# The last weight pair moves ahead of the overflow steps in a two-layer-trunk inference kernel

## Chip, core and metric

The kernel runs on one core of one Trainium2 chip. The metric is the device time in microseconds (us) of one execution; the time given for a kernel is the median of several runs. A profile is one more execution, in which the hardware records when each engine ran which instruction.

## What is computed

One inference step over 544 tokens (512 prompt tokens and 32 sample tokens, width 1024): a mixer sublayer (projections, chunk-wise spatial gating, a causal convolution with an RG-LRU scan, a sigmoid merge and an output projection), then a hierarchical mixture of experts, then a last RMS norm. The change concerns the experts:

```python
def hier_moe(x, w_rg, b_rg, w_re, b_re, w_gate, w_up, w_down):
    ...
    pg_top, g_idx = lax.top_k(pg, 1)          # one of 4 groups
    e_in = ...                                # logits of the 8 experts of that group
    pe_top, e_idx = lax.top_k(pe, TOP_K_INNER)   # 2 experts
    w = pg_top * pe_top / jnp.sum(pe_top, axis=-1, keepdims=True)
    ...
    h = jax.nn.silu(jnp.einsum('td,edf->tef', xf, w_gate)) * jnp.einsum('td,edf->tef', xf, w_up)
    h = h * gates.astype(h.dtype)[..., None]
    y = jnp.einsum('tef,efd->td', h, w_down)
```

There are 32 experts of width 256, and each token uses two of them: 1088 token places in all. The weights are float32, 3.1 MB for each expert.

## The kernel before

**Stages.** The first 375 us or so are the mixer; its weights are streamed in units and split into a high and a low part. Then the router works out on DVE (lines 1021 to 1136) which expert takes which token, and the rest of the kernel runs the experts.

**The steps of the expert stage.** Experts are run in pairs, 16 pairs (`PAIRS`) for 32 experts. A step takes a column of 128 token places: 64 (`CAP`) for the even expert, 64 for the odd one. On TensorE the two halves run side by side on 64 columns of the array each. Where an expert has more than 64 tokens, the rest goes into an extra step, in which one expert alone runs, in the first 64 places (`halves` is `(0,)`). `nx` is the number of extra steps; the router writes it and the experts concerned to `nxi`, and every engine loads it into a register once `extra_ready` is up. The column (number of the step) that a token goes to is worked out in the router: `epr` is the pair's, `xcnt[:, 2, :]` the first extra column of an expert. The extra steps stand before the last pair: columns 0 to 14 are pairs 0 to 14, columns 15 to 14 + `nx` the extras, and column 15 + `nx` is pair 15. Hence two DVE instructions (lines 1088 and 1090) add `nx` to the column of pair 15.

**One step** (`pair`, line 1437). TensorE waits for the transposed token rows `xgT` and the gate/up weights and multiplies (line 1445; 8 blocks of 128 in the contraction, the first four need part 0 of the weights, the last four part 1). With `next_rows` it then transposes the gathered rows `xg` of the next step (`transposes`, line 1429), which DVE copies to `xgT` (line 1143). Meanwhile ACT has worked out silu (line 748) and DVE the product `hm` (line 1148); TensorE transposes `hm` (line 1456), ACT copies `hT`, and TensorE multiplies with the down weights, part 2 (line 1466). ACT copies the sum to `yo` (line 753), and GpSimd scatters it by row to `ytok` in DRAM (line 553), after it has gathered the rows of the step after next (line 543). `yo` and `xg` are single buffers. Each float32 matmul of the program stands as two MATMULs in the trace.

**Weights.** There are three slots (`wslot[q]`), each of two halves (s = 0, 1), each half in three parts of 1 MB. The SP queue issues all weight transfers in the order of its program; before each part it waits until the step that uses that part of the slot is through with it: part 0 for `gu_half`, part 1 for `gu_mm`, part 2 for `pair_mm`. `refill(q, count, number)` brings two experts, `further` one. Pairs 0 to 14 use slots 0, 1, 2 in turn, the extras use half 0 of slot 0, and pair 15 slot 1. So the nine last transfers, with `nx` = 1, are: three for the extra (after pair 12 has freed slot 0), six for pair 15 (after pair 13 has freed slot 1).

**The end.** When the last scatter has landed (`yo_free`), SP loads all of `ytok` back in tiles, DVE adds them with the gates (line 1173), and the final norm and stores follow.

Of the kernel before, what the change touches and what calls it, by code (L numbers as in the profile page):

```python
# [22 lines left out]
P = 128  # L23
# [11 lines left out]
NE = NG * EG  # L35
# [4 lines left out]
PAIRS = NE // 2  # L40
# [19 lines left out]
ALU = mybir.AluOpType  # L60
# [37 lines left out]
def build(nc, x, wmix, wgate, chan, wst, bs, rows, wr, br, wmoe, y, vp, vs, st):  # L98
# [3 lines left out]
    def at(name, offset, shape, dt=F32):  # L102
# [7 lines left out]
    wslot = [[at(f"wslot{q}{s}", (first + s * 24) * K, [P, EW]) for s in range(2)]  # L110
             for q, first in enumerate((0, 97, 48))]
# [108 lines left out]
    T2 = 2 * TILES  # L220
# [4 lines left out]
    xcnt = small("xcnt", [P, 3, NE])  # L225
# [8 lines left out]
    with ExitStack() as ctx:  # L234
# [10 lines left out]
        part_in = [[[sem(f"part{n}_in{q}{s}") for s in range(2)] for q in range(3)] for n in range(3)]  # L245
# [117 lines left out]
        def _(sp_):  # L363
            e = sp_
# [68 lines left out]
            def refill(q, count, number):  # L433

                for part, used in enumerate((gu_half, gu_mm, pair_mm)):
                    lo, hi = PARTS[part]
                    e.wait_ge(used, count)
                    e.sem_inc(held, 1)
                    for s in range(2):
                        e.dma_start(wslot[q][s][:, lo:hi], wmoe[bass.ds(number + s, 1), :, lo:hi].rearrange(  # L440
                            "a p c -> (a p) c")).then_inc(part_in[part][q][s], 16)

            with e.Fori(0, 4) as i:
                for q in range(3):
                    refill(q, i * 3 + (q + 1), i * 6 + (6 + 2 * q))

            e.wait_ge(extra_ready, 1)
            nx = e.value_load(nxi[0:1, 0:1], min_val=0, max_val=EXTRA)

            def further(count, m):  # L450
                ex = e.value_load(nxi[0:1, bass.ds(m + 1, 1)], min_val=0, max_val=NE - 1)
                for part, used in enumerate((gu_half, gu_mm, pair_mm)):
                    lo, hi = PARTS[part]
                    e.wait_ge(used, count)
                    e.sem_inc(held, 1)
                    e.dma_start(wslot[0][0][:, lo:hi], wmoe[bass.ds(ex, 1), :, lo:hi].rearrange(  # L456
                        "a p c -> (a p) c")).then_inc(part_in[part][0][0], 16)

            with e.If(nx > 0):
                further(PAIRS - 3, 0)  # L460
            refill(1, PAIRS - 2, NE - 2)
            with e.If(nx > 1):
                with e.Fori(1, nx) as m:
                    further(m + (PAIRS - 1), m)
            e.wait_ge(pair_mm, PAIRS - 1)
            e.dma_start(nf[:], rows[2:3, :].broadcast_to([P, D])).then_inc(const_in, 16)

# [298 lines left out]
        def _(d):  # L766
            own = Steps(d, dve_s)
# [18 lines left out]
            for t in range(TILES):  # L786
# [6 lines left out]
                                       op0=ALU.mult, op1=ALU.mult).then_inc(xn_ready, 1)  # L793
# [22 lines left out]
            for n in (13, 11, 9, 7, 5, 3, 1):  # L816
# [5 lines left out]
                                            op0=ALU.mult, op1=ALU.add))  # L822
# [4 lines left out]
            for j in range(KT):  # L827
                h = j // 2
                d.scalar_tensor_tensor(out=bterm[:, j, :], in0=ps[:, 7, h * P:(h + 1) * P], scalar=hln[:, j, 1:2],
                                       in1=bsh[:, h, :], op0=ALU.mult, op1=ALU.add).then_inc(bt_ready, 1)  # L830
# [49 lines left out]
            for j in range(KT):  # L880
                d.wait_ge(z_mm, j + 1)
                d.scalar_tensor_tensor(
                    out=zT[:, j, 0:SEQ].rearrange("p (c t) -> p c t", c=NT),
                    in0=ps[:, ZB[j % 4], :].rearrange("p (c t) -> p c t", c=NT), scalar=hln[:, j, 0:1],
                    in1=bterm[:, j:j + 1, :].broadcast_to([P, NT, P]), op0=ALU.mult, op1=ALU.add).then_inc(z_ready, 1)
            for j in range(KT):
                d.wait_ge(z_mm, KT + 1)
                d.scalar_tensor_tensor(
                    out=zT[:, j, SEQ:TA].rearrange("p (b s) -> p b s", b=DB),
                    in0=ps[:, ZB[0], j * S:(j + 1) * S].rearrange("p (b s) -> p b s", b=DB), scalar=hln[:, j, 0:1],  # L890
                    in1=bterm[:, j:j + 1, 0:DS].broadcast_to([P, DB, DS]), op0=ALU.mult, op1=ALU.add).then_inc(z_ready, 1)
# [3 lines left out]
            with d.Fori(0, KT) as j:  # L895
# [9 lines left out]
                for t in range(3):  # L905
                    own.then(d.scalar_tensor_tensor(out=XC[:, 0:SEQ], in0=XR[:, t:t + SEQ], scalar=col(C_W0 + t),
                                                    in1=XC[:, 0:SEQ], op0=ALU.mult, op1=ALU.add))
                    i = d.scalar_tensor_tensor(out=smp(XC), in0=xrs[:, :, t:t + 4], scalar=col(C_W0 + t),
                                               in1=smp(XC), op0=ALU.mult, op1=ALU.add)
                    if t < 2:  # L910
# [35 lines left out]
                                                op0=ALU.add, op1=ALU.mult))  # L946
                own.then(d.scalar_tensor_tensor(out=M[:, SEQ:TA], in0=gbs[:], scalar=1.0, in1=XC[:, SEQ:TA],
                                                op0=ALU.add, op1=ALU.mult))
# [96 lines left out]
            for t in range(TILES):  # L1045
                i = d.tensor_tensor(cum[:, t + 1, :], cum[:, t, :], mcnt[:, t, :], ALU.add)
                if t < NT:
# [20 lines left out]
            a_ = own.mark(d.tensor_tensor(c8, bc(ps[:, 0, TILES * NE:(TILES + 1) * NE], nck), row(caps[:], NE), ALU.is_gt))  # L1068
# [3 lines left out]
            a_ = own.mark(d.reduce_sum(xcnt[:, 0, :], c8, axis=AX))  # L1072
# [3 lines left out]
            a_ = own.mark(d.tensor_tensor_scan(xcnt[:, 1, :], ones[:, 0:NE], xcnt[:, 0, :], 0.0, ALU.mult, ALU.add))  # L1076
            own.upto(b_)
            b_ = own.mark(d.tensor_tensor(c10, bc(rk[:], nck), row(caps[:], T2), ALU.is_ge))
            own.upto(a_)
            a_ = own.mark(d.scalar_tensor_tensor(out=xcnt[:, 2, :], in0=xcnt[:, 1, :], scalar=float(PAIRS - 2), in1=xcnt[:, 0, :],  # L1080
                                                 op0=ALU.add, op1=ALU.subtract))
            own.upto(b_)
            b_ = own.mark(d.reduce_sum(chk[:], c10, axis=AX))
# [1 line left out]
            a_ = own.mark(d.tensor_tensor(pick, oh10, row(xcnt[:, 2, :], T2), ALU.mult))  # L1085
            own.upto(b_)
            own.mark(d.tensor_scalar(isx[:], chk[:], 1.0, None, ALU.is_ge))
            own.then(d.scalar_tensor_tensor(out=ebx[:], in0=epr[:], scalar=PAIRS - 1.5, in1=xcnt[:, 1:2, NE - 1].broadcast_to([P, T2]),
                                            op0=ALU.is_ge, op1=ALU.mult))
            own.then(d.tensor_tensor(epr[:], epr[:], ebx[:], ALU.add))  # L1090
            own.mark(d.tensor_scalar(is0[:], chk[:], 1.0, None, ALU.is_lt))
            own.mark(d.scalar_tensor_tensor(out=posv[:], in0=chk[:], scalar=-float(CAP), in1=rk[:], op0=ALU.mult, op1=ALU.add))
            b_ = own.mark(d.tensor_tensor(colv[:], chk[:], epr[:], ALU.subtract))
# [1 line left out]
            a_ = own.mark(d.reduce_sum(ebx[:], pick, axis=AX))  # L1095
# [5 lines left out]
            a_ = own.mark(d.tensor_tensor(ebx[:], ebx[:], colv[:], ALU.add))  # L1101
# [85 lines left out]
        def _(pe):  # L1187
# [241 lines left out]
            def transposes(G):  # L1429

                pe.wait_ge(xg_in, G * 16 + 16)
                pe.wait_ge(xgT_sb, FIRST + G)
                for c in range(KT):
                    l = pe.transpose(ps[:, c // 4, (c % 4) * P:(c % 4 + 1) * P], xg[:, c * P:(c + 1) * P], ident[:])  # L1434
                l.then_inc(xgT_mm, 1)

            def pair(G, q, halves, weights_in, next_rows):
                pe.wait_ge(xgT_sb, FIRST + G + 1)
                pe.wait_ge(hm_ready, FIRST + G)
                for c in range(KT):  # L1440
                    if c % 4 == 0:
                        for s in halves:
                            pe.wait_ge(part_in[c // 4][q][s], weights_in)
                    for s in halves:
                        l = pe.matmul(ps[CAP * s:CAP * s + CAP, 2, :], xgT[:, c, CAP * s:CAP * s + CAP],  # L1445
                                      wslot[q][s][:, c * 512:(c + 1) * 512], start=c == 0, stop=c == KT - 1,
                                      tile_position=(0, CAP * s), skip_group_check=True)
                    if c == 3:
                        l.then_inc(gu_half, 1)
                l.then_inc(gu_mm, 1)  # L1450
                if next_rows:
                    transposes(G + 1)
                pe.wait_ge(hm_ready, FIRST + G + 1)
                pe.wait_ge(hT_sb, FIRST + G)
                for f in range(2):
                    l = pe.transpose(ps[:, 3, f * P:(f + 1) * P], hm[:, f * P:(f + 1) * P], ident[:])
                l.then_inc(hT_mm, 1)
                pe.wait_ge(hT_sb, FIRST + G + 1)
                for s in halves:
                    pe.wait_ge(part_in[2][q][s], weights_in)  # L1460
                pe.wait_ge(yo_sb, FIRST + G)
                for f in range(2):
                    for h in range(2):
                        for s in halves:
                            o = GU + f * D + h * 512
                            l = pe.matmul(ps[CAP * s:CAP * s + CAP, 6 + h, :], hT[:, f, CAP * s:CAP * s + CAP],  # L1466
                                          wslot[q][s][:, o:o + 512], start=f == 0, stop=f == 1,
                                          tile_position=(0, CAP * s), skip_group_check=True)
                l.then_inc(pair_mm, 1)

            transposes(0)
            with pe.Fori(0, PAIRS // 3) as i:
                for q in range(3):
                    pair(i * 3 + q, q, (0, 1), i * 16 + 16, True)
            pe.wait_ge(extra_ready, 1)
            nx = pe.value_load(nxi[0:1, 0:1], min_val=0, max_val=EXTRA)
            with pe.If(nx > 0):
                with pe.Fori(0, nx) as m:
                    pair(m + (PAIRS - 1), 0, (0,), m * 16 + 16 * (PAIRS // 3 + 1), True)
            pair(nx + (PAIRS - 1), 1, (0, 1), 16 * (PAIRS // 3 + 1), False)  # L1480


_INS = ["x", "wmix", "wgate", "chan", "wst", "bs", "rows", "wr", "br", "wmoe"]
# [54 lines left out]
```

## Time and profile before

| | |
|---|---|
| median of 3 runs | 682.99 us (682.36 to 683.5) |
| the profiled execution | 682.99 us, span of its trace 681.0 us |
| TensorE matmul busy | 572.9 us (84%) |
| DVE, ACT, GpSimd busy | 295.5, 242.6, 64.0 us |
| moved by the DMA queues | 156.31 MB, mean 230 GB/s |
| start of the first expert transposes, start of the last down burst | 403.49, 644.09 us |

The expert stage is that from about 400 to 650 us. Each busy time is a sum over stages with different limits, and matmuls overlap, so it tells nothing by itself of what bounds a stage; for that one has to see which wait ends last there.

### The profile page before, as it was taken

The numbers are of one execution on the slowest core, as the hardware profiler recorded it, in microseconds if no ns is written. First come the engines' busy times: TensorE is split into PE (matmuls) and PEld (weight loads), VectorE is DVE, ScalarE is ACT, GpSimd is POOL, SyncE is SP. The second block draws the span as 40 slices with busy tenths as digits, with TensorE's granted clock in tenths as the row PEclk, the third lists the DMA queues.
The fourth block names the chain that finished last, engine by engine and source line by source line (L and its number), as shares of the span: only waits on it lengthen the run. The fifth ranks groups of instructions, "written<-read, shape, count | busy, mean of one in ns | idle before, by whom it ended". The sixth has DMA issues, their size and how long they took to land.

```text
span 681.0 us, 8485 instructions
## 1 busy us (share of the span) xinstructions
PE 572.9 (84%) x2668; PEld 342.4 (50%) x2668; DVE 295.5 (43%) x583; ACT 242.6 (36%) x386; POOL 64.0 (9%) x137
## 2 busy tenths in 40 slices
PE   3899899999999999999998129898888988889800
PEld 3666497777778777777665113333333323223300
DVE  4824667767767667676323740110011000001138
ACT  5323324464573754654133401222222221112222
POOL 1100070000000000000000011112211221111000
PEclk9899999999999999999999659989999998889965
DMA  9322233921223222311903929999999999999464
GB/s 310 120 66 89 66 115 133 391 101 62 72 69 98 92 69 92 100 62 54 385 1 142 359 103 395 418 422 420 420 420 422 420 420 422 421 420 417 174 247 173
DMA packets 32001, 156.31 MB, mean 230 GB/s; under 512 B 6160, under 2 KB 6544, under 8 KB 19312
## 3 DMA queue, kind: packets, MB, share of 16 engines
q1 hardware_dynamic: 25744, 143.10, 53.5%
q0 software_dynamic: 5472, 10.63, 4.3%
q10 hardware_dynamic: 768, 2.38, 0.9%
q8 instruction: 9, 0.15, 0.1%
q14 instruction: 8, 0.07, 0.0%
HBM read 150.82 MB, written 14.17 MB: 242 GB/s over the span
## 4 chain that ended last, share of the span: by engine, by line
PE 55%; DMA 15%; SPq 15%; DVE 8%; issue 3%; ACT 3%; POOLq 0%; POOL 0%; DVEq 0%; ACTq 0%
PE ps L1192 13%; SPq L440 13%; PE ps L1194 12%; PE ps L1193 12%; DMA wslot<-in_wmoe 4%; DMA ytok<-yo,coly 4%; DMA xg<-xnd,colg 4%; PE ps L1466 3%; PE ps L1219 2%; PE ps L1308 2%; PE ps L1340 2%; DVE x L1173 2%; PE ps L1445 2%; SPq L456 1%; PE ps L1292 1%
## 5 line engine op out<-in xcount | busy, mean ns | idle before, releaser
L1445 PE MATMUL ps<-wslot,xgT 128*64 128x512 f32 x528 | 128.3, 621 | 11.4 <-DMA wslot<-in_wmoe 9.8
L589 ACT ACTIVATE wh<-raw 128x1024 fp32r<-128x1024 f32 x48 | 50.8, 1059 | 171.5 <-PE ps L1194 100.0
L1192 PE MATMUL ps<-xh,wh 128*128 128x512 f32 x256 | 102.5, 401 | 0.0
L1194 PE MATMUL ps<-xl,wh 128*128 128x512 f32 x256 | 100.0, 391 | 0.0
L1193 PE MATMUL ps<-xh,wl 128*128 128x512 f32 x256 | 99.9, 390 | 0.0
L1148 DVE TENSOR_TENSOR hm<-hs,ps 128x256 f32<-128x256 f32 x17 | 7.2, 421 | 197.0 <-ACT hs L748 197.0
L1445 PEld LDWEIGHTS ps<-wslot,xgT 128*64 128x64 f32 x528 | 42.2, 143 | 93.9 <-issue 93.9
L774 DVE TENSOR_TENSOR wl<-raw,wh 128x1024 fp32r<-128x1024 f32 x48 | 59.4, 1238 | 62.4 <-ACT wh L589 61.5
L1466 PE MATMUL ps<-wslot,hT 128*64 128x512 f32 x264 | 65.5, 627 | 8.3 <-ACT hT L750 8.3
L1192 PEld LDWEIGHTS ps<-xh,wh 128*128 128x128 f32 x256 | 48.1, 188 | 16.1 <-issue 6.7
L1194 PEld LDWEIGHTS ps<-xl,wh 128*128 128x128 f32 x256 | 48.1, 188 | 10.5
L1193 PEld LDWEIGHTS ps<-xh,wl 128*128 128x128 f32 x256 | 48.2, 188 | 9.4
L748 ACT ACTIVATE hs<-ps 128x256 f32<-128x256 f32 x17 | 6.5, 383 | 105.8 <-PE ps L1445 105.8
L753 ACT ACTIVATE yo<-ps 128x1024 f32<-128x1024 f32 x17 | 17.4, 1024 | 67.4 <-PE ps L1466 67.4
L1466 PEld LDWEIGHTS ps<-wslot,hT 128*64 128x64 f32 x264 | 19.2, 142 | 43.7 <-issue 31.4
L1434 PE MATMUL ps<-ident,xg 128*128 128x128 f32 x136 | 19.5, 288 | 16.9 <-DMA xg<-xnd,colg 16.9
L1434 PEld LDWEIGHTS ps<-ident,xg 128*128 128x128 f32 x136 | 15.3, 145 | 30.5 <-DMA xg<-xnd,colg 25.6
L1192 PE MATMUL ps<-wh,xh 128*128 128x512 f32 x64 | 27.3, 427 | 2.8 <-DVE xs L800 2.1
L1143 DVE TENSOR_TENSOR xgT<-ps,ch 128x1024 f32<-128x1024 f32 x17 | 20.8, 1225 | 19.5 <-PE ps L1434 19.5
L1192 PE MATMUL ps<-wh,mh 128*128 128x512 f32 x64 | 25.9, 405 | 0.2 <-DVE x L964 0.2
L1193 PE MATMUL ps<-wh,xl 128*128 128x512 f32 x64 | 26.0, 406 | 0.0
L1194 PE MATMUL ps<-wl,xh 128*128 128x512 f32 x64 | 25.9, 405 | 0.0
(290 smaller groups left out, 746.7 us busy)
## 6 DMA issues: line engine op xcount, KB each, us to landing
wslot<-in_wmoe SPq DMA_DIRECT2D x99, 1024.0 KB, 23.9
raw<-in_wmix SPq DMA_DIRECT2D x48, 512.0 KB, 3.6
gy<-ytok SPq DMA_DIRECT2D x8, 512.0 KB, 6.4
xt<-in_x SPq DMA_DIRECT2D x4, 512.0 KB, 7.1
x<-in_x SPq DMA_DIRECT2D x4, 512.0 KB, 4.8
xnd<-xn ACTq DMA_DIRECT2D x4, 512.0 KB, 9.1
out_y<-xn SPq DMA_DIRECT2D x4, 512.0 KB, 2.6
gw<-in_wgate POOLq DMA_DIRECT2D x8, 128.0 KB, 2.4
```

Source lines behind the costliest of these rows:

```text
L440: e.dma_start(wslot[q][s][:, lo:hi], wmoe[bass.ds(number + s, 1), :, lo:hi].rearrange("a p c -> (a p) c")).then_inc(part_in[part][q][s], 16)
L589: a.activation(wh[:, hslot, :], raw[:, slot, :, :].rearrange("p k c -> p (k c)"), ACT.Copy).then_inc(hi_ready, 1)
L753: a.activation(yo[:], ps[:, 6:8, :].rearrange("p b c -> p (b c)"), ACT.Copy).then_inc(yo_sb, 1)
L774: d.tensor_tensor(wl[:, hslot, :], raw[:, slot, :, :].rearrange("p k c -> p (k c)"), wh[:, hslot, :].bitcast(F32), ALU.subtract).then_inc( ...
L1143: d.tensor_tensor(xgT[:], ps[:, 0:2, :].rearrange("p b (k c) -> p (b k) c", c=P), ch[:, :, C_G2:C_G2 + 1].broadcast_to([P, KT, P]), ALU.mu ...
L1173: d.scalar_tensor_tensor(out=x1[0:r, t, :], in0=gy[0:r, s, t, :], scalar=gate[0:r, s, t:t + 1], in1=x1[0:r, t, :], op0=ALU.mult, op1=ALU.a ...
L1192: pe.matmul(out, sh, mh_, start=start, stop=False)
L1193: pe.matmul(out, sl, mh_, start=False, stop=False)
L1194: return pe.matmul(out, sh, ml_, start=False, stop=stop)
L1434: l = pe.transpose(ps[:, c // 4, (c % 4) * P:(c % 4 + 1) * P], xg[:, c * P:(c + 1) * P], ident[:])
L1445: l = pe.matmul(ps[CAP * s:CAP * s + CAP, 2, :], xgT[:, c, CAP * s:CAP * s + CAP], wslot[q][s][:, c * 512:(c + 1) * 512], start=c == 0, st ...
L1466: l = pe.matmul(ps[CAP * s:CAP * s + CAP, 6 + h, :], hT[:, f, CAP * s:CAP * s + CAP], wslot[q][s][:, o:o + 512], start=f == 0, stop=f == 1 ...
```

## The change

The order of the last steps is turned round: pair 15 is run as column 15, right behind pair 14, and the extra steps follow as columns 16 and up.

- SP: `refill(0, 13, 30)` stands right behind the loop; `nxi` is loaded after it, and the extras' weights go to half 0 of slot 1 (freed by pair 13, and from the second extra on by the extra before).
- TensorE: pair 15 runs on slot 0 without transposing the next rows; the extras run in a loop on slot 1, each with its own `transposes` ahead of its matmuls.
- Router: the first extra column is one higher, and the two DVE instructions that moved pair 15's column are gone.

```diff
             with e.Fori(0, 4) as i:
                 for q in range(3):
                     refill(q, i * 3 + (q + 1), i * 6 + (6 + 2 * q))
+            refill(0, PAIRS - 3, NE - 2)
 
             e.wait_ge(extra_ready, 1)
             nx = e.value_load(nxi[0:1, 0:1], min_val=0, max_val=EXTRA)
@@ further(count, m)
-                    e.dma_start(wslot[0][0][:, lo:hi], wmoe[bass.ds(ex, 1), :, lo:hi].rearrange(
-                        "a p c -> (a p) c")).then_inc(part_in[part][0][0], 16)
+                    e.dma_start(wslot[1][0][:, lo:hi], wmoe[bass.ds(ex, 1), :, lo:hi].rearrange(
+                        "a p c -> (a p) c")).then_inc(part_in[part][1][0], 16)
 
             with e.If(nx > 0):
-                further(PAIRS - 3, 0)
-            refill(1, PAIRS - 2, NE - 2)
-            with e.If(nx > 1):
-                with e.Fori(1, nx) as m:
-                    further(m + (PAIRS - 1), m)
+                further(PAIRS - 2, 0)
+                with e.If(nx > 1):
+                    with e.Fori(1, nx) as m:
+                        further(m + PAIRS, m)
@@ router, on DVE
-            a_ = own.mark(d.scalar_tensor_tensor(out=xcnt[:, 2, :], in0=xcnt[:, 1, :], scalar=float(PAIRS - 2), in1=xcnt[:, 0, :],
+            a_ = own.mark(d.scalar_tensor_tensor(out=xcnt[:, 2, :], in0=xcnt[:, 1, :], scalar=float(PAIRS - 1), in1=xcnt[:, 0, :],
                                                  op0=ALU.add, op1=ALU.subtract))
...
-            own.then(d.scalar_tensor_tensor(out=ebx[:], in0=epr[:], scalar=PAIRS - 1.5, in1=xcnt[:, 1:2, NE - 1].broadcast_to([P, T2]),
-                                            op0=ALU.is_ge, op1=ALU.mult))
-            own.then(d.tensor_tensor(epr[:], epr[:], ebx[:], ALU.add))
@@ TensorE, behind the loop over pairs 0 to 14
+            pair(PAIRS - 1, 0, (0, 1), 16 * (PAIRS // 3 + 1), False)
+
             pe.wait_ge(extra_ready, 1)
             nx = pe.value_load(nxi[0:1, 0:1], min_val=0, max_val=EXTRA)
             with pe.If(nx > 0):
                 with pe.Fori(0, nx) as m:
-                    pair(m + (PAIRS - 1), 0, (0,), m * 16 + 16 * (PAIRS // 3 + 1), True)
-            pair(nx + (PAIRS - 1), 1, (0, 1), 16 * (PAIRS // 3 + 1), False)
+                    transposes(m + PAIRS)
+                    pair(m + PAIRS, 1, (0,), m * 16 + 16 * (PAIRS // 3 + 1), False)
```

In the rows below, `wslot_49` and `wslot_50` are the halves 0 and 1 of slot 0, `wslot_51` and `wslot_52` those of slot 1. TensorE, behind the loop over pairs 0 to 14, in the kernel before:

```order
L1476 TENSOR_LOAD nxi
...
L1445 MATMUL ps<-wslot_49,xgT 64x512 x8
L1431 ISA
L1434 MATMUL ps<-ident,xg 128x128 x8
L1456 MATMUL ps<-ident,hm 128x128 x2
L1466 MATMUL ps<-wslot_49,hT 64x512 x4
...
L1445 MATMUL ps<-wslot_51,xgT 64x512
L1445 MATMUL ps<-wslot_52,xgT 64x512
...
L1466 MATMUL ps<-wslot_51,hT 64x512
L1466 MATMUL ps<-wslot_52,hT 64x512
```

The same place in the changed kernel:

```order
L1463 MATMUL ps<-wslot_49,hT 64x512
L1463 MATMUL ps<-wslot_50,hT 64x512
...
L1475 TENSOR_LOAD nxi
L1475 ISA x2
...
L1431 MATMUL ps<-ident,xg 128x128 x8
L1435 REGISTER_ALU
L1440 ISA
L1442 MATMUL ps<-wslot_51,xgT 64x512 x8
L1453 MATMUL ps<-ident,hm 128x128 x2
L1463 MATMUL ps<-wslot_51,hT 64x512 x4
```

The transposes of the next rows (`ident,xg`) stood between gate/up and the transposes of `hm` of the step ahead; now they stand behind the down matmuls of pair 15 and ahead of the extra's own matmuls. SP, behind the loop of refills, before:

```order
L448 TENSOR_LOAD nxi
...
L451 TENSOR_LOAD nxi
...
L456 DMA wslot_49<-in_wmoe 128x2048
...
L440 DMA wslot_51<-in_wmoe 128x2048
L440 DMA wslot_52<-in_wmoe 128x2048
```

And in the changed kernel:

```order
L440 DMA wslot_49<-in_wmoe 128x2048
L440 DMA wslot_50<-in_wmoe 128x2048
...
L449 TENSOR_LOAD nxi
...
L452 TENSOR_LOAD nxi
...
L457 DMA wslot_51<-in_wmoe 128x2048
```

Each of these transfers stands there three times, once for each part. Pair 15's six have moved ahead of the loads of `nxi` and of the extra's three.

## Rows read from the trace of the kernel before

**Rows 1.** The page: 40 slices of the span (17 us each), and steps on DVE.
```profile
GB/s 310 120 66 89 66 115 133 391 101 62 72 69 98 92 69 92 100 62 54 385 1 142 359 103 395 418 422 420 420 420 422 420 420 422 421 420 417 174 247 173
...
L1148 DVE TENSOR_TENSOR hm<-hs,ps 128x256 f32<-128x256 f32 x17 | 7.2, 421 | 197.0 <-ACT hs L748 197.0
```

**Rows 2.** The chain that ended last: start us, us, engine, tile, line.
```profile
405.50 1.24 DVE xgT L1143
407.06 8.58 PE ps L1445 x32
...
605.35 2.68 SPq L440
...
608.07 30.32 DMA wslot<-in_wmoe
...
638.53 3.67 PE ps L1445 x16
...
644.09 3.67 PE ps L1466 x16
647.78 1.03 ACT yo L753
...
650.08 3.25 DMA ytok<-yo,coly
```

**Rows 3.** Weight transfers, three windows of one issue each: issue time, time to landing.
```profile
L456 SPq DMA_DIRECT2D wslot<-in_wmoe x1: 5777/5777/5777, 593.0 to 593.0; - x1
...
DMA to landing us min/median/max: 30.6/30.6/30.6
...
L440 SPq DMA_DIRECT2D wslot<-in_wmoe x1: 1696/1696/1696, 601.4 to 601.4; - x1
...
DMA to landing us min/median/max: 28.6/28.6/28.6
...
L440 SPq DMA_DIRECT2D wslot<-in_wmoe x1: 429/429/429, 613.1 to 613.1; - x1
...
DMA to landing us min/median/max: 30.8/30.8/30.8
```

**Rows 4.** Timeline of DVE: start us, us, line, operation.
```profile
390.19 0.16 DVE L1088 SCALAR_TENSOR_TENSOR ebx<-epr,xcnt 128x10 f32<-128x10 f32 x1
...
390.59 0.17 DVE L1091 TENSOR_SCALAR is<-chk 128x10 f32<-128x10 f32 x1
...
630.42 1.23 DVE L1143 TENSOR_TENSOR xgT<-ps,ch 128x1024 f32<-128x1024 f32 x1 [0.19 <-PE ps L1434]
```

**Rows 5.** Timeline of TensorE; in brackets idle before and what ended it.
```profile
525.88 5.35 PE L1466 MATMUL ps<-wslot,hT 128*64 128x512 f32 x16 [0.47 <-ACT hT L750]
...
597.04 5.35 PE L1445 MATMUL ps<-wslot,xgT 128*64 128x512 f32 x16 [2.50 <-DMA wslot<-in_wmoe]
...
613.19 3.65 PE L1445 MATMUL ps<-wslot,xgT 128*64 128x512 f32 x16 [1.88 <-DMA wslot<-in_wmoe]
...
618.88 3.65 PE L1466 MATMUL ps<-wslot,hT 128*64 128x512 f32 x16 [0.66 <-ACT hT L750]
622.33 7.03 PE L1445 MATMUL ps<-wslot,xgT 128*64 128x512 f32 x16
629.29 1.09 PE L1434 MATMUL ps<-ident,xg 128*128 128x128 f32 x8
...
631.20 3.22 PE L1466 MATMUL ps<-wslot,hT 128*64 128x512 f32 x7 [0.47 <-ACT hT L750]
```

**Rows 6.** One stretch: us, busy time by engine, TensorE's granted clock, DMA share, GB/s.
```profile
597.00:602.40 5.40, 5.36 (x17) 1.87 (x18) 0.00 (x0) 0.00 (x0) 0.00 (x0) 0.68 1.02 425
```

**Rows 7.** DMA, 640 to 647 and 650 to 655: queue, packets, MB, share; one store.
```profile
q0 software_dynamic: 45, 0.02, 1.2%
...
q0 software_dynamic: 144, 0.33, 16.8%
...
out_st<-so ACTq DMA_DIRECT2D x1, 144.0 KB, 1.8
```

## The prediction, made before the changed kernel had run

> **What bounds the kernel now.** I read the page's slices first. From slice 25 to 37 the 16 DMA engines move 417 to 422 GB/s without a pause [rows 1]: the whole expert stage is paced by the weight transfers, and TensorE waits in it. The instruction groups show 17 steps, not 16 [rows 1]: one expert overflows, so `nx` is 1 and exactly one extra step runs, step 15 of 0 to 16. Then the chain that ended last: the late weight transfers, the second gate/up burst of pair 15 at 638.53, its down burst at 644.09, the `yo` copy at 647.78, the scatter from 650.08 [rows 2]. All that comes behind the last `yo` copy is alike in both kernels but for the size of the scatter, so the question is when the last `yo` copy can start.
>
> Landing times are issue plus time to landing [rows 3]. The nine transfers of 1 MB behind pair 14's land one after another: in the order of the queue, the second at 593.0 + 30.6 = 623.6, the fourth at 601.4 + 28.6 = 630.0, the sixth at 605.35 [rows 2] + 30.6 = 636.0, the seventh at 608.07 + 30.32 = 638.4 [rows 2], the ninth at 613.1 + 30.8 = 643.9. Before, the first three are the extra expert's and the last six pair 15's. TensorE begins pair 15's down burst at 644.09, just as its last weights land (643.9) and as its own chain (gate/up end 642.20, then silu, product, transpose, copy) comes out: weights and TensorE are level at the end of the kernel before.
>
> **The change, part by part.**
>
> *Routing.* Two small DVE instructions go. They start at 390.19, and the one behind them at 390.59 [rows 4]: 0.40 us, on the path, since TensorE, GpSimd and the first gather wait for what this chain makes. The weight stream behind it starts only when the first step frees a part of a slot, so it all moves ahead: **-0.4 us**. Bounds: 0, if something else starts the stream, and -0.4.
>
> *SP queue.* The same nine transfers go out, pair 15's six first, then the extra expert's three, and the two register loads move behind the six. No slot wait becomes late: pair 15's parts wait for pair 12 (as the extra's did), the extra's for pair 13, whose down burst ends where pair 14's gate/up begins, 3.65 + 1.88 us ahead of 613.19 [rows 5], so at 607.7, before the last of the nine goes out (613.1 [rows 3]). A transfer needs 28 to 31 us from issue to landing [rows 3], so a few us in which SP loads a register are covered by what is queued. I keep the nine landing times and only rename them: pair 15 has part 0 at 623.6, part 1 at 630.0, part 2 at 636.0; the extra has its parts at 638.4, about 641 and 643.9.
>
> *PE, pair 15 now first.* I write every time on the old clock and take off the 0.4 us at the end. Pair 14's down burst starts at 618.88, and the next thing can start 3.45 us later, at 622.33 [rows 5]. Before, that was the extra step, whose weights lay ready. Now it is pair 15, and part 0 is complete at 623.6: start 623.75 (with the 0.14 us between landing and start of the burst at 638.53 [rows 2]), end 627.4 by 3.65 us a burst [rows 5]. Part 1 is there at 630.0: TensorE idles 2.7 us and starts at 630.15. How long this burst takes is a choice. After three waits for weights, from 1.96 to 2.50 us, it took 5.35 us (the longest wait's row is shown), after 1.88 us 3.65 us [rows 5]; the mean granted clock was 0.68 from 597.0 to 602.4, so part of that burst ran at 1.2 GHz and the rest at 2.4 [rows 6]. With 2.7 us ahead of it I take 5.35: end 635.5. Down starts 1.9 us behind the end of gate/up (642.20 to 644.09 [rows 2]): 637.4, part 2 having landed at 636.0. These waits come about because the extra step, which before filled TensorE's time from 622.33 while pair 15's weights were on the way, no longer stands there.
>
> *PE, the extra step now last.* Its gather is no trouble: the rows of step 16 lay ready at 629.29 before [rows 5] and the gather is issued as before. But its transposes are no longer issued in the silu wait of the step ahead of it; they come behind pair 15's down burst. 637.4 + 3.45 = 640.8 transposes; the DVE copy to `xgT` starts 1.13 us after them (629.29 to 630.42) and takes 1.23 us [rows 4, 5]: 643.2; 0.32 us to the first matmul, as at the first step (405.50 + 1.24 to 407.06 [rows 2]): 643.5. All three of its parts but the last have landed, and that one does at 643.9. A half step is no shorter than a pair: its 16 gate/up matmuls take 7.03 us, since nothing runs beside them [rows 5], and its down burst starts 631.20 - 622.33 = 8.87 us after its beginning. So down starts at 652.35, and `yo` 3.69 us later (644.09 to 647.78 [rows 2]): 656.04 instead of 647.78, **+8.3 us**. Of this some 2.7 us are the uncovered transposes and copy, the rest waits for pair 15's weights and the slow burst. The register load, branch and semaphore instructions between the two steps are counted at nothing: the same load stood between pair 14 and the extra step, and the burst at 622.33 followed as closely as others do [rows 5]; if the array has to wait for them, up to 1 us (an estimate: three times the 0.32 us above).
>
> *Last scatter.* Now it carries the extra's rows: 0.02 MB instead of 0.33 MB [rows 7]. It took 3.25 us. The bytes themselves are 0.31 MB at 0.42 MB/us, 0.75 us; bounds are 0 and 1.45 us, the latter from the 1.8 us of an uncontended store [rows 7]. I take **-0.75 us**. The Trainium skill (DMA: Bandwidth & Descriptors, Anatomy of one DMA) gives some 2.0 us fixed plus bytes at 436 GB/s: 2.1 us for this scatter, so -1.2 us and a sum of 689.7 us; no unloaded scatter that small is in this trace.
>
> Pair 15's own scatter starts some 6 us behind 637.4 and has 12 us till the last `yo` copy needs it. ACT, DVE and GpSimd have the same programs per step.
>
> **Sum.** The profiled execution took 682.99 us, span 681.0, which is also the median of the three runs. 682.99 + 8.3 - 0.4 - 0.75 = **690.1 us**. The measurement of this kernel can tell about 0.2% (1.4 us) from no change.
>
> **The rivals.**
>
> *The clock stays full* in pair 15's second burst, as at 613.19 [rows 5]. Then it ends at 633.8, and down waits for part 2 until 636.15: 1.2 us earlier, **688.9 us**. Against it: the wait is longer than all the waits after which the burst was slow. Chance 0.18.
>
> *A second fall of the clock.* Ahead of the extra's gate/up burst TensorE idles some 1.6 us behind a short transpose group. At 525.88 a down burst took 5.35 us after such gaps [rows 5], and the first step's 32 matmuls 8.58 us where the extra's 16 take 7.03 [rows 2, 5]. It costs 1.6 us: **691.7 us**. The Trainium skill (TensorE: Matmul & The Clock Gate, HAM oscillation) says that a wait for a transfer lets the array be throttled again, so that the next burst starts cold. By that rule this is the likeliest case; the trace agrees at 597.04 and not at 613.19. Chance 0.20.
>
> *Pair 15 hardly waits*, because its parts come earlier than my renamed landings (the queue drains faster with another order). With no wait at all it has down at 631.2, transposes at 634.7, `xgT` at 637.0; the extra then waits for its part 0 (638.4, start 638.55), `yo` at 651.1: +3.3 - 1.15, **685.1 us** as the floor, most of this case 686 to 688. Against it: the same bytes lie in the same queue. Chance 0.08.
>
> *Faster.* The last transfer is 1 MB wide behind a half step, not a pair; if TensorE were always ahead, the end would be set by the landing at 643.9 in both kernels, and only the gains are left: 682.99 - 1.15 = **681.8 us**. It decides this way if the extra's gate/up starts by 635.0 (643.9 less 8.9); but part 2 of pair 15, which must be worked off first, lands at 636.0. Chance 0.02.
>
> *It doesn't do what it says*: were the overflow step not run, or run where it was, only the routing's 0.4 us would show: **682.6 us**. The trace has the overflow, and no input changes. Chance 0.02.
>
> **How the numbers follow.** Forecast 690.1 us with 0.50 (its own range 689.2 to 691.0: scatter, register load and landing times). The range reaches to the full clock on one side and the second fall on the other, with the scatter's bounds and 0.5 us of the runs' spread: 687.8 to 692.4; outside lie most of the third case, the two after it and some of the tails, under 0.2. Slower by over 0.2% are the first four: 0.96; same 0.02, faster 0.02.
>
> **What would show it.** In the profile of the changed kernel: 17 steps; DVE without the two rows; TensorE waiting for weights twice in pair 15 (about 1.4 and 2.7 us) and its second burst at 5.35; transposes of the extra behind the down burst, some 2.7 us with TensorE idle for about 1.6; the last gate/up burst 7.03 us; last `yo` copy 8 us later; last scatter 2.5 us. It is wrong if pair 15's parts land much earlier or later than renamed, if TensorE stalls on the register load, or if the weight stream no longer ends at about 643.5.

## The result, and the profile after

The changed kernel took 690.82 us (median of 4 runs, 688.38 to 691.25), the kernel before beside it 683.11 us (4 runs, 682.36 to 683.5): the ratio, 1.012 with a 95% interval of 1.0094 to 1.0147, goes by all 24 executions of the changed kernel on record (688.38 to 694.32 us, median 691.46). It is slower by 7.7 us by the four runs and by about 8.3 us by the 24; forecast were 7.1 us and 690.1 us. Where the text below says 7.7 us, it goes by the four runs. The profiled execution took 691.71 us, with a span of 690.1 us against 681.0.

The chain that ended last, from the weight transfer that was waited for to the last scatter (start us, us, engine, tile, line), answers to [rows 2]:

```profile
606.67 30.26 DMA wslot<-in_wmoe
636.93 0.25 issue
637.18 5.33 PE ps L1463 x16
642.51 1.04 PE ps L1431 x8
643.55 0.02 issue
643.58 1.23 DVE xgT L1140
644.81 0.12 issue
644.93 7.09 PE ps L1442 x16
...
653.85 3.66 PE ps L1463 x8
657.53 1.03 ACT yo L753
...
659.83 2.53 DMA ytok<-yo,coly
```

Before, the chain went from a weight transfer (landing 638.39) through one half of a gate/up burst and one down burst to the `yo` copy at 647.78. Now it goes from the landing at 636.93 through a down burst, the row transposes, the DVE copy, a whole gate/up burst of the half step and another down burst: 657.53, 9.75 us later. The last scatter is 0.72 us shorter.

TensorE over a somewhat longer stretch, with idle time and what ended it in brackets, answers to [rows 5]:

```profile
608.67 3.65 PE L1442 MATMUL ps<-wslot,xgT 128*64 128x512 f32 x16 [1.21 <-DMA wslot<-in_wmoe]
614.92 3.65 PE L1442 MATMUL ps<-wslot,xgT 128*64 128x512 f32 x16 [2.60 <-DMA wslot<-in_wmoe]
...
620.88 3.65 PE L1463 MATMUL ps<-wslot,hT 128*64 128x512 f32 x16 [0.94 <-DMA wslot<-in_wmoe]
625.76 3.65 PE L1442 MATMUL ps<-wslot,xgT 128*64 128x512 f32 x16 [1.22 <-DMA wslot<-in_wmoe]
630.93 3.65 PE L1442 MATMUL ps<-wslot,xgT 128*64 128x512 f32 x16 [1.51 <-DMA wslot<-in_wmoe]
635.51 0.44 PE L1453 MATMUL ps<-ident,hm 128*128 128x128 f32 x2 [0.93 <-DVE hm L1145]
637.18 5.33 PE L1463 MATMUL ps<-wslot,hT 128*64 128x512 f32 x16 [1.24 <-DMA wslot<-in_wmoe]
642.45 1.09 PE L1431 MATMUL ps<-ident,xg 128*128 128x128 f32 x8
644.93 7.08 PE L1442 MATMUL ps<-wslot,xgT 128*64 128x512 f32 x16 [1.39 <-DVE xgT L1140]
```

In pair 15 (from 625.76) TensorE waits three times for weights, then for the copied rows. The slow burst is the down burst at 637.18, not the second gate/up burst: that one took 3.65 us. The burst at 614.92 took 3.65 us after a wait of 2.60 us, longer than the 2.50 us of [rows 5] after which one took 5.35. Pair 14 is later too: its down burst waits 0.94 us for weights and starts at 620.88; before, it waited for none and started at 618.88 [rows 5].

DVE where the two instructions stood, answering to [rows 4]:

```profile
390.67 0.17 DVE L1087 TENSOR_SCALAR isx<-chk 128x10 f32<-128x10 f32 x1
390.74 0.17 DVE L1088 TENSOR_SCALAR is<-chk 128x10 f32<-128x10 f32 x1
```

The next instruction now starts 0.07 us behind `isx`; before, `isx` started at 390.11 and that instruction at 390.59 [rows 4]: 0.48 us. So 0.41 us are gone there.

### The profile page after: what moved, and what is told of

Same layout as the page of the kernel before. It is cut to its first block, busy times and chain, and to the rows that moved or that the text cites. A ratio compares the mean times of both kernels' runs of the same rounds, so it can differ in the third digit from the quotient of the medians.

```text
span 690.1 us, 8482 instructions
## 1 busy us (share of the span) xinstructions
PE 572.9 (83%) x2668; PEld 341.1 (49%) x2668; DVE 296.2 (43%) x581; ACT 242.6 (35%) x386; POOL 64.9 (9%) x137
## 4 chain that ended last, share of the span: by engine, by line
PE 53%; SPq 15%; DMA 15%; DVE 10%; issue 3%; ACT 3%; POOLq 0%; POOL 0%; DVEq 0%; ACTq 0%
SPq L440 14%; PE ps L1189 12%; PE ps L1191 12%; PE ps L1190 12%; DMA wslot<-in_wmoe 4%; DMA xg<-xnd,colg 4%; DMA ytok<-yo,coly 4%; PE ps L1463 3%; PE ps L1305 2%; PE ps L1442 2%; PE ps L1337 2%; PE ps L1216 2%; DVE x L1170 2%; PE ps L1431 1%; PE ps L1289 1%
## 5 line engine op out<-in xcount | busy, mean ns | idle before, releaser
L1442 PE MATMUL ps<-wslot,xgT 128*64 128x512 f32 x528 | 126.9, 617 | 19.0 <-DMA wslot<-in_wmoe 16.0
```

## Experiments

The theory: three things are in the loss. The row transposes and the copy of the extra step lie uncovered (2.6 us), pair 15 waits for weights because the step that filled that time has gone behind it, and a burst of pair 15 runs partly at 1.2 GHz. Against it stand the routing and the smaller scatter. Rivals: the weight stream alone sets the end; the transposes are all of the loss; it is something else in the new program (the order of the transfers, branches, register loads).

### The rows of the extra step transposed early

```diff
-            pair(PAIRS - 1, 0, (0, 1), 16 * (PAIRS // 3 + 1), False)
             pe.wait_ge(extra_ready, 1)
             nx = pe.value_load(nxi[0:1, 0:1], min_val=0, max_val=EXTRA)
+            pair(PAIRS - 1, 0, (0, 1), 16 * (PAIRS // 3 + 1), False, nx)
             with pe.If(nx > 0):
-                with pe.Fori(0, nx) as m:
-                    transposes(m + PAIRS)
...
+                pair(PAIRS, 1, (0,), 16 * (PAIRS // 3 + 1), False)
@@ in pair, behind the gate/up matmuls
+                if first_extra is not None:
+                    with pe.If(first_extra > 0):
+                        transposes(G + 1)
```

> The changed kernel, with the transposes of the first extra step's rows issued in pair 15's silu wait again (the register load moves ahead of pair 15). Theory (the loss is uncovered row transposes and copy, waits for pair 15's weights, and a slow burst): the extra's gate/up burst follows pair 15's down burst at once, so 2.4 to 2.7 us less than the changed kernel: about 688.3 us. Rival (the end is set by the weight stream, TensorE's order doesn't matter): no change, 690.8 us. Rival (all of the loss is the uncovered transposes): 683 us.

Measured: 687.04 us (7 runs), the kernel before beside it 684.23 us (22 runs); ratio 1.0041 (1.0022 to 1.0059). It is 2.8 us over the kernel before, where the changed kernel is 7.7 us over it: 4.9 us less, more than was expected (4.4 by the second measurement of the changed kernel, further down). Its trace is the changed kernel's to within 0.1 us up to pair 15's down burst; TensorE from there:

```profile
634.52 1.09 PE L1431 MATMUL ps<-ident,xg 128*128 128x128 f32 x8
635.52 0.44 PE L1456 MATMUL ps<-ident,hm 128*128 128x128 f32 x2
637.18 3.65 PE L1466 MATMUL ps<-wslot,hT 128*64 128x512 f32 x16 [1.22 <-DMA wslot<-in_wmoe]
640.63 7.03 PE L1442 MATMUL ps<-wslot,xgT 128*64 128x512 f32 x16
...
649.50 3.65 PE L1466 MATMUL ps<-wslot,hT 128*64 128x512 f32 x8 [0.47 <-ACT hT L750]
```

Both down bursts start at 637.18, but this one takes 3.65 us and not 5.33, and the extra's burst starts at 640.63 and not at 644.93. Of these 4.3 us, 1.7 are the burst and 2.6 the transposes and copy. So the two rivals fall: the order on TensorE matters, and the transposes are a part only, since 2.8 us of loss remain. Moved into the idle time, they also leave TensorE idle for less of it, and here the clock stayed up: the granted clock from 625 to 645 us was 1.00, in the changed kernel 0.91. That the shorter idle time is what kept it up is argued here; the fills below test it.

### The weights back in the old order

```diff
-            refill(0, PAIRS - 3, NE - 2)
             e.wait_ge(extra_ready, 1)
             nx = e.value_load(nxi[0:1, 0:1], min_val=0, max_val=EXTRA)
...
                 further(PAIRS - 2, 0)
+            refill(0, PAIRS - 3, NE - 2)
```

> The changed kernel, but SP sends the extra's three weight transfers first and pair 15's six behind them, as before; TensorE runs pair 15 first all the same. Theory: pair 15's parts land at 633.5, 638.4 and 643.9 instead of 623.6, 630.0 and 636.0, its down burst starts at 644.1 and the last yo copy at about 662.5: 6.5 us more than the changed kernel, about 697.3 us. Rival (order of the transfers is nothing, the stream only has to end): 690.8 us.

Measured: 697.94 us (4 runs) beside the same 684.23: 13.7 us over the kernel before, 6.0 more than the changed kernel (6.5 were expected). TensorE:

```profile
632.54 9.98 PE L1442 MATMUL ps<-wslot,xgT 128*64 128x512 f32 x32 [8.31 <-DMA wslot<-in_wmoe]
643.46 0.44 PE L1453 MATMUL ps<-ident,hm 128*128 128x128 f32 x2 [0.93 <-DVE hm L1145]
644.37 3.65 PE L1463 MATMUL ps<-wslot,hT 128*64 128x512 f32 x16 [0.47 <-ACT hT L750]
...
650.44 7.08 PE L1442 MATMUL ps<-wslot,xgT 128*64 128x512 f32 x16 [1.40 <-DVE xgT L1140]
```

Pair 15 finds its weights 8.31 us late, its 32 gate/up matmuls take 9.98 us instead of 7.04, so a part of them ran at 1.2 GHz, and its down burst starts at 644.37, about where the last down burst of the kernel before starts (644.09); the extra step comes on top. The landing of pair 15's weights sets when pair 15 runs, and the changed SP order is what keeps the loss from being 13.7 us.

### Both kernels with a shorter weight stream

Of pair 14's second expert only 16 of the 2048 columns of each part are loaded, so the weight stream is 3 MB shorter; this is done once in the kernel before and once in the changed one:

```diff
                     for s in range(2):
-                        e.dma_start(wslot[q][s][:, lo:hi], wmoe[bass.ds(number + s, 1), :, lo:hi].rearrange(
+                        end = lo + 16 if light and s else hi
+                        e.dma_start(wslot[q][s][:, lo:end], wmoe[bass.ds(number + s, 1), :, lo:end].rearrange(
...
-            with e.Fori(0, 4) as i:
+            with e.Fori(0, 3) as i:
                 for q in range(3):
                     refill(q, i * 3 + (q + 1), i * 6 + (6 + 2 * q))
+            for q in range(3):
+                refill(q, 9 + q + 1, 18 + 6 + 2 * q, q == 2)
```

> The kernel before, but of pair 14's second expert only 16 columns of each part are loaded (its output is wrong for that), so the weight stream is 3 MB shorter, some 7.5 us. Theory: TensorE no longer waits for weights in pairs 14 and 15 and sets the end; by the rows of before pair 14's down burst starts at 616.6 instead of 618.9 and the last down burst at 641.0 instead of 644.1: 3 us less, about 680.0 us. Rival (the stream alone sets the end): 7.5 us less, 675.6 us.

> The changed kernel with the same 3 MB less (pair 14's second expert, output wrong for that). Theory: pair 15 finds its weights and hardly waits; what is left against the other kernel with the short stream is the uncovered transposes and copy (+2.7), less the routing and the scatter (-1.15), so +1.5 to 2 us against it: about 681.8 us. Rival (the loss has nothing to do with waits for weights): still +7.7 us against it, 687.7 us.

Measured, both beside the kernel before at 684.23 us: the kernel before with the short stream 682.92 us (10 runs, ratio 0.998, 0.9968 to 0.9993), the changed kernel with it 682.65 us (10 runs, 0.9978, 0.9961 to 0.9995). The difference of 7.7 us is gone; forecast were +1.5 to +2 us between the two, and here there was none (the second measurement of the changed one, further down, came out higher). The traces show what is between. First the kernel before with the short stream, then the changed one:

```profile
609.21 7.04 PE L1448 MATMUL ps<-wslot,xgT 128*64 128x512 f32 x32
...
621.59 7.03 PE L1448 MATMUL ps<-wslot,xgT 128*64 128x512 f32 x16
630.22 1.09 PE L1437 MATMUL ps<-ident,xg 128*128 128x128 f32 x8 [1.60 <-DMA xg<-xnd,colg]
```

```profile
608.46 7.04 PE L1445 MATMUL ps<-wslot,xgT 128*64 128x512 f32 x32
...
620.83 7.04 PE L1445 MATMUL ps<-wslot,xgT 128*64 128x512 f32 x32
...
633.30 1.09 PE L1434 MATMUL ps<-ident,xg 128*128 128x128 f32 x8
635.79 7.08 PE L1445 MATMUL ps<-wslot,xgT 128*64 128x512 f32 x16 [1.39 <-DVE xgT L1143]
```

Without waits for weights in pairs 14 and 15 TensorE comes to the row transposes of step 16 before GpSimd's gather has landed: 1.60 us of waiting in the kernel before. The changed order needs those rows a step later and has no such wait. Of its 2.6 us for uncovered transposes and copy 1.0 is left, less the 0.7 us of the scatter and what the routing brings; the traces agree, with 39.9 us from pair 14's gate/up to the last `yo` copy (608.46 to 648.39) against 38.9 (609.21 to 648.08). That also tells why the kernel before gained 1.3 us from the short stream and not 3. The waits for weights, with the fall of the clock that came with them (pair 15's down burst is back at 3.65 us in this trace of the changed kernel), are thus a cause of the loss, shown by taking away what was waited for; the times of both kernels with the short stream also carry the effect of the gather.

### Both edits together

The early row transposes and the short stream in the changed kernel, with the changed kernel with the short stream beside it once more.

> Both at once: the extra's rows transposed in pair 15's silu wait and the stream 3 MB shorter (pair 14's second expert, output wrong for that). Theory A (the uncovered 2.6 us and the waits for weights add up, nothing else is in the loss): 2.6 us less than the changed kernel with the short stream. Theory B, from the trace of the kernel before with the short stream, where TensorE waited 1.60 us for the gathered rows: the row transposes now stand in the time in which that gather is still under way, so 1.5 of the 2.6 us come back as a wait for the gather, and it is about 1 us less.

> The changed kernel with the short stream once more (pair 14's second expert, output wrong for that), beside the kernel with both edits: the last yo copy at 36.9 us behind the start of pair 14's gate/up burst minus 3 (39.9 us in its first trace, 608.46 to 648.39), that is again about 39.9 us; with both edits 38.9 us by theory B, 37.3 us by theory A.

Measured beside the kernel before at 683.49 us (19 runs): with both edits 680.23 us (8 runs, ratio 0.9951, 0.9935 to 0.9968), with the short stream alone 684.49 us (12 runs, 1.0007, 0.999 to 1.0024). The early rows bring 4.3 us here, more than the 2.6 of theory A and the 1 of theory B. From pair 14's gate/up to the last `yo` copy it is 38.1 us with both edits (607.54 to 645.7, where the last down burst ends), between the 37.3 of theory A and the 38.9 of theory B. TensorE with both edits:

```profile
619.91 7.04 PE L1445 MATMUL ps<-wslot,xgT 128*64 128x512 f32 x32
627.84 1.09 PE L1434 MATMUL ps<-ident,xg 128*128 128x128 f32 x8 [0.90 <-DMA xg<-xnd,colg]
...
633.11 7.03 PE L1445 MATMUL ps<-wslot,xgT 128*64 128x512 f32 x16
```

and with the short stream alone, in this second execution:

```profile
623.99 3.65 PE L1445 MATMUL ps<-wslot,xgT 128*64 128x512 f32 x16 [0.31 <-DMA wslot<-in_wmoe]
628.57 0.44 PE L1456 MATMUL ps<-ident,hm 128*128 128x128 f32 x2 [0.93 <-DVE hm L1148]
629.88 5.35 PE L1466 MATMUL ps<-wslot,hT 128*64 128x512 f32 x16 [0.87 <-DMA wslot<-in_wmoe]
```

The gather wait of theory B is there, but 0.90 us long; against the first trace of the kernel with the short stream (39.9 us) the stretch is 1.8 us shorter, between the two theories. My expectation that the stretch of the changed kernel with the short stream would repeat at 39.9 us failed: it took 42.6 us (607.68 to 650.24), since a down burst went to 5.35 us here and short waits for weights were back. Between the two traces of this pair of kernels the step from pair 15's down burst to the extra's gate/up burst is 3.49 us with the early rows (629.62 to 633.11) and 7.76 without (629.88 to 637.64): again 2.6 us of transposes and copy and 1.7 of the burst, as above.

The changed kernel with the short stream alone is thus 1.6 us under the kernel before in one measurement and 1.0 us over it in the other, so the difference between the two kernels with the short stream is known only roughly: none to some 2.3 us. Against the kernel before, both edits come out 3.3 us faster, the kernel before with the short stream, measured on another chip, 1.3 us. That the new order is the better one where the weights are there in time and the rows transposed early is therefore suggested, not shown; by the traces its stretch is 0.8 us shorter (38.1 against 38.9) and its scatter 0.7. In the real kernel the weights aren't there.

### Something to do for TensorE in its idle time

```diff
+            def fill(n):
+                for _ in range(n):
+                    pe.matmul(ps[:, 4, :], ident[:], wsT[:].rearrange("p h t -> p (h t)"), start=True, stop=True)
...
                     if c % 4 == 0:
+                        fill(fills[c // 4])
...
+                fill(fills[2])
...
-            pair(PAIRS - 1, 0, (0, 1), 16 * (PAIRS // 3 + 1), False)
+            pair(PAIRS - 1, 0, (0, 1), 16 * (PAIRS // 3 + 1), False, (1, 1, 1))
```

The three numbers are the fills ahead of pair 15's first and second gate/up burst and its down burst.

> The changed kernel, with three full matmuls of 128x512 whose result nobody reads (bank 4) put into pair 15's idle time: one ahead of its first gate/up burst, one ahead of the second, one ahead of the down burst. Theory (in the changed kernel's trace pair 15's down burst takes 5.33 us because the clock fell in the idle time ahead of it): the burst takes 3.65 us, the later steps start 1.7 us earlier, about 1.5 us less than the changed kernel beside it. Rival (the long burst has another cause, such as the branch code behind it): no change, or 0.9 us more where a fill delays a burst.

> The changed kernel unchanged, on the chip of the fill kernel, to stand beside it: about 7.7 us over the kernel before. If its down burst of pair 15 is at 3.65 us in this trace, the burst's length varies between executions and the fill has to be judged by the runs; if at 5.3 us, the fall belongs to this order.

Measured beside the kernel before at 684.18 us (11 runs): with fills 690.17 us (6 runs, ratio 1.0081, 1.0066 to 1.0095), without 691.36 us (6 runs, 1.01, 1.0078 to 1.0122). The two intervals overlap, so the times alone (1.2 us less with fills) don't settle it. The traces: with fills, then without:

```profile
616.21 3.65 PE L1447 MATMUL ps<-wslot,xgT 128*64 128x512 f32 x16 [2.33 <-DMA wslot<-in_wmoe]
...
638.62 3.65 PE L1469 MATMUL ps<-wslot,hT 128*64 128x512 f32 x16 [0.35 <-DMA wslot<-in_wmoe]
```

```profile
614.54 3.65 PE L1442 MATMUL ps<-wslot,xgT 128*64 128x512 f32 x16 [2.64 <-DMA wslot<-in_wmoe]
...
636.77 5.32 PE L1463 MATMUL ps<-wslot,hT 128*64 128x512 f32 x16 [1.24 <-DMA wslot<-in_wmoe]
```

The same stretch of both (us, busy time of PE, PEld, DVE, ACT, POOL, granted clock, DMA share, GB/s), with fills first:

```profile
636.00:643.00 7.00, 5.72 (x29) 2.54 (x28) 0.42 (x1) 1.46 (x3) 0.00 (x0) 1.00 0.46 193
```

```profile
636.00:643.00 7.00, 6.23 (x24) 2.45 (x24) 0.00 (x0) 0.87 (x1) 0.00 (x0) 0.76 0.34 140
```

With the fills the granted clock is 1.00 (2.4 GHz) throughout and the burst 3.65 us; without, 0.76 on average, so part of it ran at 1.2 GHz. The weights of the fill kernel came 1.9 us later in its execution, which is why the last `yo` copies are level in these two traces; 1.7 us of that were there in pair 14 (616.21 against 614.54), ahead of the first fill. From that burst to the last `yo` copy it is 41.1 us with fills (to 657.29) and 42.6 without (to 657.12): 1.5 us less, as expected. The long burst is a matter of the clock, not of the branches behind it, and it costs 1.7 us on TensorE.

## Why the prediction was right, and where it was off

- **What bounds.** Right for the end of the stage, which is all that the sum uses. That the weights pace the whole expert stage and TensorE waits in it for them is not so: in the trace of the kernel before TensorE waits for weights from the burst at 557.83 on; from 405 to 556 us it waited 9.2 us for gathered rows and never for weights, though the transfers ran at 418 to 422 GB/s from 425 us on [rows 1]. At the end TensorE and the weights were level, and moving a step from ahead of the wait to behind it put its length on the path.
- **Renamed landings.** Nearly right. Pair 15's landings came at 625.6 (592.2 + 33.4), 630.8 (602.0 + 28.8) and 636.93 instead of 623.6, 630.0 and 636.0. I had taken pair 14 over unchanged, but its weights came later as well (its down burst started 2.0 us later); why is open, and in the trace with the old queue order pair 14's down burst didn't wait for weights. Here is the second landing, with its time to landing:

```profile
L440 SPq DMA_DIRECT2D wslot<-in_wmoe x1: 2108/2108/2108, 602.0 to 602.0; - x1
...
DMA to landing us min/median/max: 28.8/28.8/28.8
```

  The experiment with the old order shows that the order in the queue sets when a step's weights land.
- **Waits.** The first wait was 1.22 us (predicted 1.4), the second 1.51 (2.7), and a third of 1.24 ahead of the down burst that I had not on the path. In sum 4.0 against 4.1 us. The second was shorter because part 0 landed 2.0 us later than forecast and part 1 only 0.8.
- **The slow burst.** Its size was right (1.7 us), its place wrong. I put it into the second gate/up burst, where 0.5 us of it would have been hidden by part 2's landing; it was the down burst, which hides nothing. I had derived it from how long the wait right ahead of it was, and the row at 614.92 shows that this doesn't decide. The rival of full clock had the second gate/up burst right, but not the down burst behind it; that of a second fall failed: there was one fall, and the extra's gate/up burst, 1.39 us of waiting ahead of it, took 7.08 us.
- **Uncovered transposes and copy.** Right: 2.6 us in the traces of the early rows.
- **The half step.** Right: 7.08 us, down burst 8.92 us behind its start (8.87).
- **Register load and branches at nothing.** Right: transposes start at 642.45, 5.27 us behind the start of a burst of 5.33.
- **Scatter.** Right: 2.53 against 2.50 us. By the Trainium skill (DMA: Bandwidth & Descriptors, Anatomy of one DMA) it would have been 2.1, an estimate from its fixed cost and bytes; the measurement decides, and the rows were nearer.
- **Routing.** The 0.41 us are gone on DVE. That they come out at the end is not shown: in these traces the first expert transposes start anywhere from 402.74 to 405.10 us, the kernel before (403.49) and the same with the short stream (404.41) lying between kernels that lack the two instructions.
- **Sum.** The last `yo` copy was expected at 656.04, with the routing's 0.4 us not yet taken off, and came at 657.53; the 1.5 us too few are mainly the last landing (0.9) and the place of the slow burst (0.5). With the 0.4 us of the routing, which this execution doesn't show, they make the 1.9 us by which its span of 690.1 us lies over the forecast of 688.2 (681.0 + 7.15). The median of the four runs lies 0.7 us over the forecast, that of all 24 executions 1.4 us: the mechanism was right, and that the first number fits so well is in part luck.

The Trainium skill (TensorE: Matmul & The Clock Gate, HAM oscillation) says that a wait for a transfer lets the array be throttled again. The fills, which take only the idle time away, agree for pair 15; the bursts at 614.92 and 630.93, at full speed right behind such waits, show that not each wait does it. Where the prediction called a second fall the likeliest case by that rule, the trace disagrees.

## What to carry to other kernels

Where TensorE and a transfer stream are level, the step whose data already lie ready belongs ahead of the wait, not behind it; the smallest step isn't the best last one merely because it moves least. A step that is taken out of a pipelined loop loses its prefetch: the transposes of its rows and the copy behind them must be put back by hand, and here they were worth 2.6 us and, by keeping TensorE from idling, 1.7 more. Before an order is changed, ask what comes last once the wait that came last is gone: with the weights in time it was the gather, for which TensorE then waited 0.9 to 1.6 us.

## What was not expected of the hardware

The clock's fall doesn't follow the last wait. In the kernel before, a burst took 5.35 us after 2.50 us of waiting; in the changed kernel one took 3.65 after 2.60 us and another 5.33 after 1.24 us, with three more gaps of 0.93 to 1.51 us in pair 15 ahead of it. In one of the two executions of the changed kernel with the short stream pair 15's down burst took 5.35 us, in the other 3.65. Filling the gaps with three matmuls that nobody reads kept the granted clock at 1.00 from 625 to 645 us (0.91 without), and the bursts behind them took 3.65, 3.66 and 3.65 us.
